# Fox attention: the order of the query tiles within a pair of heads

## The reference

```python
def forgetting_attention(q, k, v, c):
    for blk in range(t // BLOCK_Q):                 # BLOCK_Q = 128
        q0 = blk * BLOCK_Q
        q1 = q0 + BLOCK_Q
        s = jnp.einsum('bqhd,bkhd->bhqk', q[:, q0:q1], k[:, :q1]).astype(jnp.float32) * ATTN_SCALE
        s = s + c_h[:, :, q0:q1, None] - c_h[:, :, None, :q1]
        causal = jnp.arange(q1)[None, :] <= (q0 + jnp.arange(BLOCK_Q))[:, None]
        s = jnp.where(causal, s, NEG_INF)
        p = jax.nn.softmax(s, axis=-1).astype(v.dtype)
        outs.append(jnp.einsum('bhqk,bkhd->bqhd', p, v[:, :q1]))
```

## Time and profile before

| | us |
|---|---|
| median of three runs | 2982.47 (2975.87 to 2986.69) |
| the profiled execution | 2981.84 |
| its span, first to last instruction | 2980.0 |
| busy PE / DVE / ACT / POOL over the span | 2788.6 / 1863.9 / 1202.4 / 1311.8 |
| fox phase, first scores on PE | 1950.58 |
| fox phase, start of the last store operations on DVE | 2166.27 |

### The profile page before, as it was taken

One profiled execution on the slowest core, in us unless ns is written; L12 is line 12 of the kernel. 1 busy time (PEld: TensorE's weight loads), 2 busy tenths in 40 slices (PEclk: granted clock), 3 DMA queues, 4 the chain that ended last, 5 costly groups with the idle time before them and its releaser, 6 DMA issues. The chain is left out here.

```text
span 2980.0 us, 56718 instructions
## 1 busy us (share of the span) xinstructions
PE 2788.6 (94%) x23069; PEld 2243.1 (75%) x23069; DVE 1863.9 (63%) x2523; ACT 1202.4 (40%) x2178; POOL 1311.8 (44%) x1116
## 2 busy tenths in 40 slices
PE   7999989989799999998999899988889999999898
PEld 5888777777667788887887777756667788887787
DVE  6333566666444755566986788867752765556895
ACT  3111343333233433334434766545542433334442
POOL 6344234444222545457554454432112555455653
PEclk9999899999799999999999899999999999999999
DMA  5333100010131233336542233342122233335651
GB/s 198 114 93 104 59 25 25 25 46 4 30 121 64 85 122 112 114 113 211 164 117 89 57 100 93 110 158 86 65 79 85 77 120 106 109 113 173 189 143 67
DMA packets 290601, 295.37 MB, mean 99 GB/s; under 512 B 11622, under 2 KB 223708, under 8 KB 289192
## 3 DMA queue, kind: packets, MB, share of 16 engines
q1 hardware_dynamic: 288440, 286.89, 30.5%
q10 hardware_dynamic: 1424, 4.83, 0.4%
q0 software_dynamic: 480, 0.03, 0.0%
HBM read 200.30 MB, written 88.65 MB: 97 GB/s over the span
## 5 line engine op out<-in xcount | busy, mean ns | idle before, releaser
L312 POOL TENSOR_TENSOR w_lo_b<-w_raw_b,w_hi_b 128x512 fp32r<-128x512 f32 (+3 forms) x540 | 748.4, 1388 | 671.0 <-ACT w_hi_b L346 667.7
L396 PE MATMUL ps<-b_hi,w_hi_b 128*128 128x512 f32 x1540 | 611.0, 397 | 13.7 <-issue 13.7
L396 PE MATMUL ps<-b_lo,w_hi_b 128*128 128x512 f32 x1540 | 603.4, 392 | 0.0
L396 PE MATMUL ps<-b_hi,w_lo_b 128*128 128x512 f32 x1540 | 602.9, 391 | 0.0
L346 ACT ACTIVATE w_hi_b<-w_raw_b 128x512 fp32r<-128x512 f32 (+3 forms) x498 | 295.5, 597 | 462.9 <-PE ps L3362 194.6
L396 PEld LDWEIGHTS ps<-b_hi,w_hi_b 128*128 128x128 f32 x1540 | 291.9, 190 | 78.8 <-issue 18.6
L396 PEld LDWEIGHTS ps<-b_lo,w_hi_b 128*128 128x128 f32 x1540 | 291.7, 189 | 64.0 <-issue 3.9
L396 PEld LDWEIGHTS ps<-b_hi,w_lo_b 128*128 128x128 f32 x1540 | 291.5, 189 | 61.6
L3362 PE MATMUL ps<-b_hi,w_hi_b 128*128 128x512 f32 x616 | 245.2, 398 | 28.6 <-DVE x_res L3182 28.0
L3362 PE MATMUL ps<-b_lo,w_hi_b 128*128 128x512 f32 x616 | 241.8, 393 | 0.0
L3362 PE MATMUL ps<-b_hi,w_lo_b 128*128 128x512 f32 x616 | 241.5, 392 | 0.0
(11 more groups left out here) (429 smaller groups left out, 5789.5 us busy)
## 6 DMA issues: line engine op xcount, KB each, us to landing
w_raw_b<-in_w_gate_up SPq DMA_DIRECT2D x88, 512.0 KB, 4.3
act_dram<-x_res SPq DMA_DIRECT2D x44, 512.0 KB, 6.0
sum_dram<-x_res SPq DMA_DIRECT2D x40, 512.0 KB, 2.9
w_raw_b<-in_w_down SPq DMA_DIRECT2D x28, 512.0 KB, 6.3
stage<-sum_dram SPq DMA_DIRECT2D x54, 256.0 KB, 3.7
stage<-act_dram SPq DMA_DIRECT2D x50, 256.0 KB, 4.3
w_raw_a<-in_a_w_in SPq DMA_DIRECT2D x23, 512.0 KB, 4.8
u_dram<-evac_a SPq DMA_DIRECT2D x16, 512.0 KB, 3.0
```

The costliest lines, as they stand in the source:

```text
L312: nc.gpsimd.tensor_tensor(self.wlo[:, r, 0:n, :], source, self.whi[:, r, 0:n, :].bitcast(F32), ALU.subtract).then_inc(self.w_lo, 1)
L396: mm = self.nc.tensor.matmul(self.ps[:, bank, :], w[:, r, k, :], h[:, block, k, :], start=(start and k == 0 and a == 0 and h is self.bh), ...
```

## The change

One line becomes two: the order of the tiles is 3, 7, 2, 6, 1, 5, 0, 4 for the first five pairs and 3, 7, 2, 6, 1, 5, 4, 0 for the last. In key tiles that is 4, 8, 3, 7, 2, 6, 1, 5, and in the last pair 4, 8, 3, 7, 2, 6, 5, 1.

```diff
-            units = [(p, t) for p in range(PAIRS) for t in (7, 3, 6, 2, 5, 1, 4, 0)]
+            tiles = [(3, 7, 2, 6, 1, 5, 0, 4)] * (PAIRS - 1) + [(3, 7, 2, 6, 1, 5, 4, 0)]
+            units = [(p, t) for p in range(PAIRS) for t in tiles[p]]
```

## The result

| | before | after |
|---|---|---|
| median (14 runs each) | 2982.78 us | 2989.56 us |
| ratio | | 1.0032 (1.0021 to 1.0044) |
| fox phase, first scores to end of the last store | 216.57 us | 227.77 us |
| period of a pair | 34.76 us | 36.25 us |

The new order is slower by 0.32%, with an interval from 0.21 to 0.44%; the prediction had 0.28% and a time of 2990.8 us. The ratio is that of the fast runs (two of before's 14, of 3196.56 and 4811.26 us, are left out) and not the quotient of the two medians, which differ by 6.8 us or 0.23%. In the profiled executions the phase is 11.2 us longer but the span only 5.3 (2985.3 against 2980.0): the phase began 3.6 us earlier, and what lies behind it was 2.3 shorter. Neither stretch has anything changed in it.

What follows compares the result with a forecast made beforehand. It took a chain alternating between PE and DVE, neither running without a break, to bound the phase. Head -1.32, four periods of +1.52 and last pair +3.57 gave +8.3 us: 2990.8 us against the median, range 2982 to 2998.

Steps and rivals of the forecast that it cites:

- The steps of a pair: Times between first reductions of successive rows (query tiles named by key tiles): sum 36.28 us against 34.76 before.
- The cause: Shares move from wide rows' reductions into narrow rows' steps, with long scores queued behind: 1.52 us more per pair.
- the shares: After every fourth row DVE forms the reciprocal and PE spreads it (1.02 us) before writing the next scores.
- The head: From the phase's first scores to the second pair's first reduction: 37.93 us, 1.32 less, as a short row fills sooner.
- The rival on the clock: PE's full clock comes late in the first pair, after broken work: +11.2 us, total 2993.7 us; chance 0.14.
- The last pair: From the last pair's first reduction to its last store: 41.85 us against 38.28, 3.57 more.
- a lateness without a known cause: The very last row began late before, with no cause in the trace: 0.34 us added to the last pair.
- the longer values: At the end, the 6-row's values, no longer the 2-row's, stand between the 5-row's turnings: 0.87 us added.
- The prediction's own band for the sum: Reading errors of the small terms put the phase's added time at 6.8 to 9.8 us, around +8.3.
- within 0.3%: Outcome that the whole kernel's time changes by no more than about 8.9 us: chance 0.57.
- slower: Outcome that the whole kernel slows by more than the line of 8.9 us: chance 0.40.
- The neutral rival: PE is the bound, so order is neutral; only head and tail terms remain: 2982.1 us; chance 0.14.

Runs made afterwards that it cites:

- turned orders: Each order started one place on, so group borders move: new order from its 8-row, period 35.09 us (new 36.25); old from its 4-row, 35.82 (old 34.76).
- new_again: The changed kernel profiled once more, nothing altered, to check the clock: period 36.23 us, phase 226.98 us; timed once at 2983.42 us.
- kernel with filler: New order plus 8 and 10 constant transposes on PE ahead of the second and third rows' scores: period 36.24 us, head 36.86, phase 225.11.
- defer_new: New order with PE's spread put behind the next row's scores and DVE's gate scaling ahead of the store: period 34.08 us, phase 214.15 us.
- head_only: Only the first pair in a new order (4, 8, 3, 7, 2, 6, 5, 1), the others old: period 34.76 us, head 42.34, phase 220.74.

## Why the prediction was right, point by point

**The steps of a pair** held to 0.1 us each: forecast 6.40, 4.61, 4.77, 4.01, 5.88, 6.98 (3.39 and 3.59) and 3.63; measured 6.39, 4.61, 4.78, 4.00, 5.78, 6.98 and 3.71. The sum was 36.28, the measure 36.25. The period grows by 1.49, not 1.52. The method that did this: in each step find which engine's chain ends last, take the nearest old step, and add or take off tiles.

**The cause** was right as to its main part. Of 1.49 us, 1.09 goes with the shares (runs without them), and the turned orders give 1.06 and 1.16 by an independent way. The prediction put all of it down to the shares; 0.33 to 0.40 is the cycle of rows itself. "Any order that alternates wide and narrow holds the same such terms, so the order alone changes little" held as "little", not as nothing. The forecast steps had this part in them without my seeing it, since each was built from its own old neighbour. The runs without the shares tell where it lies: 4 to 8 and 2 to 6 take 8.74 us there, against 8.16 for 8 to 4 and 6 to 2, and the six other steps together 0.18 less than the old ones.

**The head** was the term that failed. Forecast 37.93 us, a gain of 1.32; measured 39.49 and 40.40 in two traces, against 39.25 before, so a loss of 0.24 to 1.15. Up to the reduction of the first 8-row it held (forecast 8.05 us, measured 8.06 in the trace of after); what is missing stands in 3 to 7, 1.47 above its later length, and in 8 to 3, 0.11 above. The step that failed is the one that let the clock rise as before because the first unbroken work was as long: it did rise, but PE then idled 2.2 us (2.7 in new_again) for the reductions of the 8-row and worked at half clock once more. The rival on the clock had named this stretch, though for another reason: it had the clock not risen at all by then. Against the forecast it cost 1.6 us in the trace of after and 2.5 in that of new_again, where the two steps are 2.94 longer, as the rival's 2.9 had it. The kernel with filler does not pay it. The rival's chance of 0.14 was too low.

**The last pair** was forecast at 41.85, of which 0.34 was a lateness without a known cause and 0.87 the longer values (the terms as listed add up to 41.82). Measured 41.67, with 3.74 from 5-row to last row (forecast 3.73) and 8.13 to the end (8.17). The lateness stands in all ten traces with shares whose last row is the one-tile row, and in neither of the two without shares (5 to 1 takes 3.12 and 3.39 there). So it goes with the shares; by what wait is open.

**What was not in the sum**: the dip of the clock at the border, 1.62 us in the trace of after and none in new_again.

Together, in the trace of after: head +0.24, the four periods +5.95 with +1.62 from the dip, last pair +3.39: +11.2 us against +8.3 forecast. Without the dip it would be +9.6, and new_again has +10.4. The prediction's own band for the sum was 6.8 to 9.8, which both traces exceed, one by the dip and one by the head. The ratio says +9.5 (6.3 to 13.1), which can't tell these from the forecast. So the time came out closer than its sum: in the trace of after, the stretches outside the phase, with nothing changed in them, were 5.9 us shorter than before, and that agreement is luck. The prediction had given "within 0.3%" 0.57 and "slower" 0.40; the result of 0.32% lies just over that line, and its interval lies across it.

**The neutral rival** ("PE is the bound, the order makes no difference") is refuted by the two couples of kernels with turned orders, which have the same work on PE and differ by 1.06 and 1.16 us per pair.

## What to carry to other kernels

Where engines work in lockstep, an order of tiles can't be judged by itself: what counts is what stands behind the periodic extra work (here a spread of 1.02 us), and in whose idle time it falls. Look for the engine's own idle time in the same step and move the trigger ahead of it: moving each group's reciprocal ahead of one reduction took 1.65 us from each pair, more than the change of order had added (1.49). A short tile first fills the pipeline sooner, but behind the pause that it leaves on PE the clock may fall again.

## What the runs showed of the hardware

The time ahead of the changed phase scatters more than the change: the phase's first scores came between 1942.39 and 1957.65 us in these traces, though nothing before them differs; four traces of one chip (new_again, defer_new and the two turned orders) span that whole range. The phase alone could be read to 0.02 us per period. For changes of 0.3% the phase's own length is the better measure, and the ratio of the kernels' times only says whether it reaches the end.

PE's clock fell for 3 to 4 us in the middle of the phase, behind waits of PE as short as 0.78 us, at two of fifteen borders in three traces of the new order and at one of ten in the traces of before and head_only. The granted clock fell to 0.50 (0.55 to 0.57 over the stretches that a view was cut to), with runs of matmuls about 1.5 to 1.8 times as long, at a price of 1.1 to 1.6 us each time.
